# Second net: its first up tile behind each mixer as one fp32 product of the un-normed residual, normed afterwards; exponents of HGRN and GLA between the last token tiles

## The reference, cut to what matters

```python
for i in range(4):
    m = mixer_i(x)                       # gdn, hgrn2, gla, gdn: in-projection, scan over chunks, gated norm, @ w_out
    x = layer_norm(DN_ALPHA * x + m, mix_ln_g[i], mix_ln_b[i])
    gate, up = jnp.split(x @ ffn_w_in[i], 2, axis=-1)        # 2 x 2816 columns
    x = layer_norm(DN_ALPHA * x + (silu(gate) * up) @ ffn_w_down[i], ffn_ln_g[i], ffn_ln_b[i])

def layer_norm(x, g, b):
    mu = mean(x); var = mean((x - mu) ** 2)
    return (x - mu) * rsqrt(var + 1e-5) * g + b
```

## Time and profile before

| | us |
|---|---|
| three runs | 2440.2, 2442.35, 2442.55 (median 2442.35) |
| the profiled execution | 2440.08 |
| its span | 2438.4 |
| TensorE busy | 2379.8 |
| VectorE busy | 1754.9 |
| ScalarE busy | 1179.3 |

### The profile page before, as it was taken

One profiled execution on the slowest core, in us unless ns is written; L12 is line 12 of the kernel. 1 busy time (PEld: TensorE's weight loads), 2 busy tenths in 40 slices (PEclk: granted clock), 3 DMA queues, 4 the chain that ended last, 5 costly groups with the idle time before them and its releaser, 6 DMA issues.

```text
span 2438.4 us, 49464 instructions
## 1 busy us (share of the span) xinstructions
PE 2379.8 (98%) x19026; PEld 2200.1 (90%) x19026; DVE 1754.9 (72%) x2902; ACT 1179.3 (48%) x1828; POOL 77.1 (3%) x149
## 2 busy tenths in 40 slices
PE   8999999999999999999999999999989999999998
PEld 6877877778998999988999998999989999988998
DVE  5788799988857876776666867665567657677665
ACT  5454522223655444566444555444555446566444
POOL 1000000000000000000400000000000000000000
PEclk9999999999999999999999999999999999999999
DMA  8433355555434555422555532555425554313553
GB/s 318 156 113 121 106 192 185 189 175 168 172 105 142 195 180 177 133 74 96 190 185 188 170 105 79 191 184 191 151 90 161 189 175 155 120 62 113 199 180 130
DMA packets 119715, 378.31 MB, mean 155 GB/s; under 512 B 11655, under 2 KB 29063, under 8 KB 119184
## 3 DMA queue, kind: packets, MB, share of 16 engines
q1 hardware_dynamic: 107040, 328.62, 40.9%
q0 software_dynamic: 12528, 47.62, 5.9%
HBM read 375.15 MB, written 1.05 MB: 154 GB/s over the span
## 4 chain that ended last, share of the span: by engine, by line
PE 78%; DVE 11%; issue 6%; ACT 3%; DMA 1%; DVEq 1%; SPq 0%; ACTq 0%
PE gb L610 20%; PE gb L611 20%; PE gb L612 20%; DVE w_lo L579 2%; PE mb L719 1%; DVE W L1629 1%; PE mb L612 1%; PE mb L611 1%; PE mb L610 1%; ACT w_hi L571 1%; DMA X<-in_x 1%; PE gb L3007 1%; DVE W L1253 1%; DVE W L1254 1%; PE gb L691 1%
## 5 line engine op out<-in xcount | busy, mean ns | idle before, releaser
L610 PE MATMUL gb<-Xs,w_hi 128*128 128x256 f32 (+1 forms) x3422 | 1035.8, 303 | 10.2 <-DVE w_lo L579 5.0
L612 PE MATMUL gb<-Xs,w_lo 128*128 128x256 f32 (+1 forms) x3422 | 1022.3, 299 | 0.0
L611 PE MATMUL gb<-Xs,w_hi 128*128 128x256 f32 (+1 forms) x3336 | 992.2, 297 | 0.0
L571 ACT ACTIVATE w_hi<-raw 128x1024 fp32r<-128x1024 f32 x582 | 610.4, 1057 | 679.9 <-PE gb L612 640.7
L579 DVE TENSOR_TENSOR w_lo<-raw,w_hi 128x1024 fp32r<-128x1024 f32 x582 | 705.4, 1222 | 210.0 <-ACT w_hi L571 199.7
L610 PEld LDWEIGHTS gb<-Xs,w_hi 128*128 128x128 f32 x3422 | 645.4, 189 | 57.7 <-issue 17.4
L612 PEld LDWEIGHTS gb<-Xs,w_lo 128*128 128x128 f32 x3422 | 645.2, 189 | 26.1
L611 PEld LDWEIGHTS gb<-Xs,w_hi 128*128 128x128 f32 x3336 | 629.2, 189 | 23.4 <-issue 1.9
L611 PE MATMUL gb<-Fs,w_hi 128*128 128x256 f32 (+1 forms) x966 | 277.7, 288 | 0.0
L610 PE MATMUL gb<-Fs,w_hi 128*128 128x256 f32 (+1 forms) x880 | 248.2, 282 | 0.7 <-ACT Pj L1778 0.7
L612 PE MATMUL gb<-Fs,w_lo 128*128 128x256 f32 (+1 forms) x880 | 247.2, 281 | 0.0
(11 more groups left out here) (472 smaller groups left out, 3230.9 us busy)
## 6 DMA issues: line engine op xcount, KB each, us to landing
raw<-in_up SPq DMA_DIRECT2D x264, 512.0 KB, 3.5
raw<-in_down SPq DMA_DIRECT2D x96, 512.0 KB, 3.7
R<-in_mod_later POOLq DMA_DIRECT2D x80, 512.0 KB, 3.8
raw<-in_gdn_in SPq DMA_DIRECT2D x64, 512.0 KB, 3.5
raw<-in_down SPq DMA_DIRECT2D x48, 384.0 KB, 4.0
raw<-in_hgrn_in SPq DMA_DIRECT2D x32, 512.0 KB, 4.4
raw<-in_ev_in SPq DMA_DIRECT2D x24, 512.0 KB, 4.2
raw<-in_gla_in SPq DMA_DIRECT2D x24, 512.0 KB, 4.0
```

The lines of the kernel that those rows point to most:

```text
L571: nc.scalar.activation(hi, raw[:, slot, 0:hi.shape[1]] if len(hi.shape) == 3 else like(raw[:, slot], hi), ACT.Identity).then_inc(*hi_ready ...
L610: nc.tensor.matmul(to, weight_block(w_slot, 0, k), x_hi, start=start, stop=False)
L611: nc.tensor.matmul(to, weight_block(w_slot, 0, k), x_lo, start=False, stop=False)
L612: return nc.tensor.matmul(to, weight_block(w_slot, 1, k), x_hi, start=False, stop=stop)
```

## The change

Behind each of the four mixers of the second net:

- the five unread products go (`warm=0`);
- the first up tile is not split. SyncE loads it raw into two rows of `Pj`, and TensorE multiplies it in fp32 (8 products of 258 columns, L1122 of the new code) with rows that ScalarE makes: the residual times the norm's gain, one row behind each square (L1114), and the columns 257 and 258 are gain and bias. It goes into bank 0 of `mb`, not into `gb`;
- the norm is applied to its result afterwards (`dve_late_norm`: two operations of one column, two of 256; the bias goes into the silu). ScalarE keeps the mean for it in one more copy (L1204);
- `pe_group` takes tiles 1, 2, 3, and tile 4 finds bank 0 free. `Ahead` skips tile 0, so every split runs one tile further; VectorE makes one more low part before the norm;
- the first pair of up tiles is peeled out of the loops of VectorE and ScalarE.

In HGRN and GLA, exponents of unit 0 are issued between the two pairs of the last four token tiles, into `mb` in place of `gb`, and what ScalarE and VectorE do with them follows there. In HGRN alone, the values of chunks 0 to 3 are issued ahead of the last unit's scores, and the group norm's sums of the first two quarters together behind chunk 5.

The core of the diff (context lines left out):

```diff
@@ -365,6 +369,10 @@
+        FIRST_LATE = [first_of[name] for name in (f"up_2_{i}" for i in range(4)) if name in first_of]
+        first_raw = Pj[:, 20:22, :].rearrange("p r (b n) -> p r b n", b=4)
+        for g in FIRST_LATE:
+            kinds[g] = "late"
...
@@ -443,6 +451,19 @@
+                if start in FIRST_LATE:
+                    for t in (1, 2, 0, 3, 4, 5, 6, 7):
+                        if t:
+                            load(first + t, 0, t % SLOTS, used(start + t - SLOTS))
+                        else:
+                            sp.wait_ge(gemm_out.sem, start - KC + AHEAD)
+                            sp.dma_start(first_raw.rearrange("p r b n -> p (r b n)"), src[first]).then_inc(*first_loaded.inc(16))
+                    start += n
+                    continue
...
@@ -547,6 +568,8 @@
+                if self.at + self.n in FIRST_LATE:
+                    self.skip(1)
...
@@ -661,7 +684,10 @@
-            if ready:
+            if gain:
+                pe_gained(pe)
+                pe_group(pe, 1, n, ready)
+            elif ready:
...
@@ -669,17 +695,19 @@
-            for u in range(AHEAD if ready or by_seq else 0, peel):
+            for u in range(SLOTS if gain else AHEAD if ready or by_seq else 0, peel):
-        def pe_tokens(pe, tiles, n):
+        def pe_tokens(pe, tiles, n, halfway=None):
+                    if u and halfway:
+                        halfway()
...
@@ -878,6 +906,8 @@
+                if mixer is not None:
+                    act_gained(act, "mix", mixer, m)
...
@@ -1073,6 +1103,36 @@
+        GN = T + 2
+        def act_gained(act, which, i, m):
+            if m == 0:
+                at = VC[f"{which}_g"]
+                both = vec[:, at:at + VC[f"{which}_b"] - at + 32].rearrange("p (a c) -> p c a", a=2)
+                nc.scalar.activation(Pj[:, 0:KC, T:GN], both[:, KC * i:KC * i + KC, :], ACT.Identity)
+            nc.scalar.activation(Pj[:, m, 0:T], X[:, m, 0:T], ACT.Identity, scale=ln_gain(which, i, m)[0]).then_inc(*gain_rows.inc())
+        def pe_gained(pe):
+            pe.wait_ge(*first_loaded.due("pe", 16))
+            gemm_taken.free("pe")
+            for k in range(KC):
+                pe.wait_ge(*gain_rows.due("pe"))
+                last = nc.tensor.matmul(mb[:, 0, 0:GN], first_raw[:, k // 4, k % 4, :], Pj[:, k, 0:GN], start=k == 0, stop=k == KC - 1)
+            last.then_inc(*gemm_out.inc())
+        def dve_late_norm(dve):
+            acc, mean, to = mb[:, 0, :], W[:, 2, T:2 * T], W[:, 6, 0:T]
+            dve.wait_ge(*gemm_out.due("dve"))
+            nc.vector.tensor_scalar(small[:, 158:159], acc[:, T:T + 1], -1.0, None, ALU.mult).then_inc(*dve_step.inc())
+            nc.vector.tensor_copy(small[:, 159:160], acc[:, T + 1:T + 2])
+            dve.wait_ge(*dve_step.sent())
+            dve.wait_ge(*mean_kept.due("dve"))
+            link(dve, nc.vector.scalar_tensor_tensor(out=to, in0=mean, scalar=small[:, 158:159], in1=acc[:, 0:T], op0=ALU.mult, op1=ALU.add))
+            nc.vector.tensor_tensor(to, to, W[:, 3, T:2 * T], ALU.mult).then_inc(*late_normed.inc())
...
@@ -1140,6 +1200,8 @@
+            if which == "mix":
+                nc.scalar.activation(W[:, 2, T:2 * T], mb[:, 2, 0:T], ACT.Identity, scale=1.0 / D).then_inc(*mean_kept.inc())
...
@@ -1177,6 +1239,9 @@
+            if mixer is not None:
+                nc.vector.memset(small[:, 158:159], 0.0).then_inc(*gemm_taken.inc())
+                dve_tile(dve)
...
@@ -1255,16 +1325,17 @@
+                    if late:
+                        dve_late_norm(dve)
+                    else:
+                        dve_tile(dve)
+                        here = gemm_out.due("dve")
...
-                    dve_tile(dve)
+                    if not peeled or late:
+                        dve_tile(dve)
-                    g = W[:, 4 + u, 0:n]
+                    g = W[:, 6 if late else 4 + u, 0:n]
...
@@ -1273,22 +1344,31 @@
+            def pair(first=False):
+                    if first and u == 0:
+                        gemm_out.due("act", 2)
+                        split_hi(act, ahead["act"].next())
+                        act.wait_ge(*late_normed.due("act"))
+                        nc.scalar.activation(W[:, 6, 0:n], W[:, 6, 0:n], ACT.Silu, bias=small[:, 159:160]).then_inc(*silu_done.inc())
+                        gemm_taken.due("act", 2)
+                        continue
...
@@ -1298,9 +1378,11 @@
-            with repeat(act, FC // 2 - last, *act_counts, (silu_done, "sent", 2), *(((conv_done, "act", 2),) if conv else ())):
+            if gain:
+                pair(first=True)
+            with repeat(act, FC // 2 - last - gain, *act_counts, (silu_done, "sent", 2), *(((conv_done, "act", 2),) if conv else ())):
-            ahead["act"].skip(4 * (FC // 2 - last - 1))
+            ahead["act"].skip(4 * (FC // 2 - last - 1 - gain))
...
@@ -2569,7 +2651,7 @@
-            pe_out(pe, T, lambda k: None if k % 2 else pe.wait_ge(*gn_applied.due("pe")), layer_norm=True, aside=OUT_ASIDE)
+            pe_out(pe, T, lambda k: None if k % 2 else pe.wait_ge(*gn_applied.due("pe")), layer_norm=True, warm=0, aside=OUT_ASIDE)
...
@@ -2999,10 +3081,10 @@
-                    if u and h % 2 == 0:
+                    if u > 1 and h % 2 == 0:
-                        to = gb[:, h, t * T:(t + 1) * T].rearrange("p (a c) -> p a c", a=2)
+                        to = (gb if u else mb)[:, h, t * T:(t + 1) * T].rearrange("p (a c) -> p a c", a=2)
...
@@ -3043,37 +3125,51 @@
-            pe.wait_ge(*gemm_taken.seen("pe"))
-            pe.wait_ge(*gate_lo.due("pe"))
-            pe.wait_ge(*level_ready.seen("pe") if z.name == "gla" else level_ready.due("pe"))
-            exponents(0)
+            w = D // z.heads
+            early = KC // 2 if len(z.units) > 4 else 0
+            def value(c):
+                h, off = c * P // w, c * P
+                to = gb[:, c // 2, (c % 2) * T:(c % 2 + 1) * T]
+                first = z.rows[:, 2 * h:2 * z.heads + h + 1:2 * z.heads - h, :]
+                nc.tensor.matmul(to.rearrange("p (a i) -> p a i", a=2), z.v[:, 0, off:off + P], first, start=True, stop=False)
+                last = nc.tensor.matmul(to[:, P:T], z.v[:, 1, off:off + P], z.rows[:, 2 * h + 1, :], start=False, stop=True)
+                if early and c == early:
+                    last.then_inc(*head_out.inc(early // 2))
+                elif c % 2 and c >= early:
+                    last.then_inc(*head_out.inc())
+            def first_exponents():
+                pe.wait_ge(*gate_lo.due("pe"))
+                pe.wait_ge(*level_ready.seen("pe") if z.name == "gla" else level_ready.due("pe"))
+                exponents(0)
+            pe_tokens(pe, 4, T, halfway=first_exponents)
+            pe.wait_ge(*spans_exp.due("pe", 2))
+            pe.wait_ge(*gemm_taken.seen("pe"))
+                if u == len(z.units) - 1:
+                    pe.wait_ge(*spans_exp.due("pe", 2))
+                    for c in range(early):
+                        value(c)
-            pe.wait_ge(*spans_exp.due("pe", 2))
-            w = D // z.heads
-            for c in range(KC):
-                h, off = c * P // w, c * P
-                to = gb[:, c // 2, (c % 2) * T:(c % 2 + 1) * T]
-                first = z.rows[:, 2 * h:2 * z.heads + h + 1:2 * z.heads - h, :]
-                nc.tensor.matmul(to.rearrange("p (a i) -> p a i", a=2), z.v[:, 0, off:off + P], first, start=True, stop=False)
-                last = nc.tensor.matmul(to[:, P:T], z.v[:, 1, off:off + P], z.rows[:, 2 * h + 1, :], start=False, stop=True)
-                if c % 2:
-                    last.then_inc(*head_out.inc())
-                    if c > 1:
-                        gn_sums(pe, (c // 2 - 1,), z.parts)
+            for c in range(early, KC):
+                value(c)
+                if c % 2 and c > 1:
+                    gn_sums(pe, range(0 if c == early + 1 else c // 2 - 1, c // 2), z.parts)
-            pe_out(pe, T, lambda k: None if k % 2 else pe.wait_ge(*gn_applied.due("pe")), layer_norm=True, aside=OUT_ASIDE)
+            pe_out(pe, T, lambda k: None if k % 2 else pe.wait_ge(*gn_applied.due("pe")), layer_norm=True, warm=0, aside=OUT_ASIDE)
...
@@ -3092,17 +3188,18 @@
-            for u in range(len(z.units)):
+            def exps(u):
-                                         gb[:, 2 * b:2 * b + 2, :].rearrange("p c (t l i) -> p l (c t) i", t=2, l=2), ACT.Exp,
+                                         (gb if u else mb)[:, 2 * b:2 * b + 2, :].rearrange("p c (t l i) -> p l (c t) i", t=2, l=2), ACT.Exp,
-                if u == 0:
-                    for _ in range(2):
-                        split_hi(act, ahead["act"].next())
+            act_last_tokens(act, [z.v[:, :, 2 * T:3 * T], z.v[:, :, 3 * T:4 * T]], lambda: exps(0))
+            for u in range(1, len(z.units)):
+                exps(u)
...
@@ -3160,7 +3257,11 @@
+            dve_tile(dve)
+            dve_tile(dve, 2)
+            gemm_out.due("dve", 4)
```

(57 more changed lines are left out.)

25 lines of the change are left out of this document (10 added, 15 removed).

## The result

The changed kernel takes 2421.72 us (median of 6, 2419.2 to 2423.85) against 2442.11 (median of 6, 2440.2 to 2443.91): 20.4 less, ratio 0.9915, 95% interval 0.9905 to 0.9926. A second set beside other experiments gave 2420.45 and 0.9921 (0.9907 to 0.9936). The forecast was 2423, with 2416 to 2431.

The account below looks back on a forecast made before the run. TensorE, busy 98% of the span, was taken as the bound, with time only in its waits and unread work. Boundaries 12.2, GLA 2.0, HGRN's front 0.6 and tail 3.9 sum to 18.7 us: 2423 forecast, range 2416 to 2431.

Parts of the forecast that it names:

- The boundary: Behind each of four mixers: one tile moves into the unread products' time, 3.05 us earlier each, 12.2 in all.
- The step of the fp32 tile: At each boundary: eight fp32 products of 258 columns take 0.432 us each, 3.46 in all.
- the norm would be 0.17 late: At the boundary: the last square's gain row on ScalarE, 0.589 us, makes L1131 start 0.17 late.
- waits for bank 1: At the boundary: tile 5 needs the bank that the late pair frees, and starts after a wait of 0.6 us.
- HGRN's front: Before exponents(0) in HGRN: only the wait of 0.75 us goes, of which 0.6 was taken.
- GLA's front: In GLA: exponents(0) between the token pairs gain 0.75 + 2.16 - 0.94 = 2.0 us.
- HGRN's tail: Four early values fill a 2.01 us wait: gain 4.7 at full clock, 0.5 at the lower; 3.9 taken.
- rival 1: HGRN's tail stays at the lower clock: gain 0.5 instead of 3.9, 2427 us; chance 0.22.
- The sign that the prediction names: In HGRN: the first product after the group norm comes 4 to 5 us earlier relative to the last unit but one.
- Rival 4: At each boundary the clock falls, +8.0 us each, 2468 us in all; chance 0.06, half with fewer boundaries hit.
- Rival 3: At the boundary the late pair holds bank 1, up to 1.8 us: gain 1.3 each, 2430.5 us; chance 0.05.
- Rival 2: Elsewhere, lower-clock stretches vanish or arise: two or three fewer 2419 us (chance 0.07), two or three more 2428.

Follow-up runs that it names:

- the cores alone: The change's HGRN and GLA edits without the fp32 first tile, five unread products kept, against the kernel before: 2432.34 us, ratio 0.9965.
- the change's second trace: The changed kernel run once more, nothing altered, in a second set: 2420.45 us, ratio 0.9921 against the kernel before.
- experiment 4: The kernel before with four unread products in place of five behind the four mixers, no tile moved: 2440.08 us, ratio 0.9996.
- both parts alone: Two runs against the kernel before: only the fp32 first tile at the boundaries, 2428.03 us; only the HGRN and GLA edits, 2432.34 us.
- experiment 3: The kernel before with the unread products behind the four mixers left out and nothing put there: 2447.51 us, ratio 1.0022.

## Why the prediction was right, point by point

**The boundary.** Forecast 3.05 each, 12.2 in all; measured 3.07, 3.3, 3.4 and 3.4, 13.1. The step of the fp32 tile held: 0.435 a product, 3.48 for the eight, forecast 3.46. The estimate with the Trainium skill's four passes ("FP8 and Floating Point Precision", section "TensorE Precision Notes") was 3.72, and the trace decides for less. What was off is the estimate's measure, a split product counted as one pass, and not the four: see the last section. That the norm would be 0.17 late did not happen: the gain row takes 0.49 to 0.50, not the 0.589 of L1141, and L1166 starts 1.79 behind the last residual, L1106 did 1.78. The extra low part is hidden. The group starts 0.72 earlier on the chain (5.26 behind the last residual, 5.98 before), forecast 0.61; at the 74th product 0.2 to 0.27 is left of it, forecast 0.38, since the norm's pace sets it: with four unread products and with none the group starts at the same 5.25. Tile 5 starts 0.34 to 0.37 behind tile 4's last product at three boundaries and 0.74 at the first; less the 0.12 of a product, it waits for bank 1 0.22 to 0.25 and 0.62, forecast 0.6 at all four. This is the term that made 3.05 too small. At the first boundary VectorE's operations are longer (L1337 0.48 and L1338 0.53, at the other three 0.30 and 0.43); it is the only one where GpSimd works, which is not shown to be the cause.

**HGRN's front.** Forecast 0.6, measured 1.0. **GLA's front.** Forecast 2.0, measured 2.3. Both steps held. About 0.15 of the difference in each is a matter of reading: a row's idle time counts from the end of the row ahead, which is 0.27 to 0.28 long, while the next product can start 0.12 behind its start. The last token product of HGRN before starts 1.02 ahead of the exponents' 1436.76, so the wait was 0.90 and not 0.75. The rest was not followed.

```profile
1435.74 0.27 PE L693 MATMUL gb<-w_lo,Xs 128*128 128x256 f32 x1
```

**HGRN's tail.** Forecast 4.7 at the full clock, of which 3.9 was taken because part might run at the lower one; 2.1 in the first trace, 3.8 in the second and in the cores alone, both wholly at the full clock. So at the full clock the working is 0.9 too high, and that 3.9 comes out is luck. The mechanism was right, but one step was not: the values were to start where TensorE has no more work, and they stand behind a wait for VectorE's placing of unit 5's scores (`banks_free(u - 2)`; the first unit is 0). It costs 0.72 in the change's second trace; from the last four values to the first out product it takes 7.9 (1474.64 to 1482.58), as forecast. TensorE in that trace:

```profile
1467.18 0.70 PE L3117 MATMUL mb<-R,M 128*32 128x32 f32 x32 [0.38 <-DVE M L3227]
1468.60 0.70 PE L3135 MATMUL gb<-R,Pj 128*128 128x256 f32 x2 [0.72 <-DVE R L3254]
...
1474.64 0.67 PE L3135 MATMUL gb<-R,Pj 128*128 128x256 f32 x2 [0.99 <-DVE R L3257]
```

In the first trace the clock fell at 1469.5, 0.35 after the first value had started, and was back at 1472.9. From 1467 to 1469 TensorE had worked 1.03 us, nearly all of it on products of 16 and 32 columns.

```profile
1467.00:1469.00 2.00, 1.03 (x71) 0.82 (x60) 1.90 (x4) 0.33 (x1) 0.00 (x0) 1.00 0.03 8
1471.00:1472.00 1.00, 1.00 (x5) 0.81 (x5) 1.00 (x2) 0.00 (x0) 0.00 (x0) 0.50 0.00 0
```

This was rival 1, in part; the low stretch in HGRN's tail went from 10.2 us to 3.4, or to none. The sign that the prediction names, a first out product 4 to 5 us earlier, did not come (2.1 and 3.8).

**HGRN's middle.** No term of the sum: 2.1 us that I took for a part of the core which the change doesn't touch. It is real, since a middle of 28 came in both traces of before and in none of the other kernels. It is a side effect and not what the change does, since one unread product fewer removes it as well (experiment 4); what it comes from is open. For this forecast it is chance, neither foreseen nor needed: without it some 18.3 of the 20.4 are left. With it both parts alone gain more than their sum leaves room for: 13.9 + 9.6 = 23.5, less the 2.1 that is counted in both, 21.4, against 20.4.

**GLA's tail.** Forecast unchanged. It was 1.2 longer in the first trace (6.8 us at 0.50 in place of 3.4) and unchanged in the second.

**The sum.** In the first trace: boundaries 13.1, HGRN 1.0 + 2.1 + 2.1, GLA 2.3 - 1.2, less 3.3 ahead of the first boundary, 16.1 of the 16.2 by which the spans differ. The medians differ by more, 20.4, since the profiled execution of the change, 2423.85, was the slowest of its six and that of before was 2.0 below its median. The four terms of the forecast came to 18.5 in the first trace (13.1 + 1.0 + 2.3 + 2.1) and to 20.2 in the second, against 18.7; the middle, in no term, adds 2.1, and GLA's tail takes 1.2 or nothing. So the forecast's own terms hold: the boundaries were 0.9 and the fronts 0.7 too small, and the tail's gain varies by 1.7 with the clock. The tail's 3.9 is near by luck.

**Rival 4**, a low clock at each boundary, did not come about in the change and did in experiment 3, where TensorE idled instead. There it cost less than the rival's price: 1.0 to 2.1 per boundary, as the low stretches were 3.4 to 6.8 long and not the whole group. **Rival 3**, the late pair holding the bank by 1.8, was 0.2 to 0.6. **Rival 2** came about in part: the 6.8 us at 0.50 near 966 took 3.3 in the first trace and nothing in the second.

## What to carry to other kernels

Where an engine runs filler to keep its clock, look for real work that needs only inputs that are there: a linear norm can be applied to the product afterwards, and one product of higher price may be moved there if it fits the filler's time. Leaving the filler out was not the alternative here (5.5 us more); measure that too. Compare stages by rows inside one trace, since low-clock stretches in untouched stages move whole traces by 3 us, as much as a part of the change is worth.

## What was not expected

- One unread product fewer, hundreds of microseconds ahead, removes a loss of 2.1 us from HGRN's middle. The DMA view of before shows nothing but three instruction loads (0.05 MB) from 1440 to 1456, one of them in the slice at 1448.4, just ahead of the gap. Over all thirteen traces TensorE has eight gaps of over 1 us (1.5 to 2.1) for which the profile shows no releaser, all in the cores of HGRN and GLA, and each ends 2.3 to 2.9 us after an instruction load of 16 KB began (before: 1448.4 and 1451.04). Every trace has such loads there, the eight without such a gap too. That late instruction loading is the cause is argued from this, not shown.
- An fp32 product of 258 columns takes 0.435, 3.7 times a split product of 256 (0.117). In cycles of 2.4 GHz that is 4.0 a column for fp32, the same for the unread products of 512 columns (4.29 / 5), and 1.1 for the split product. So the ratio is under four since the split product takes more than one cycle a column; what adds the 0.1 was not followed.
- Between the two traces of the change the stretch from the last residual behind gdn0 to HGRN's gate takes 276.0 and 278.3 us, with no clock below 1.00 and one wait over 0.3 us in each, before tile 5 (0.5 and 0.6); the median distance of products is 0.117 and 0.118. What makes this 1% is open.
